# A block of ones for the key squares: one edit to the last layer and the mixers of a five-part network on one core

## The reference, cut to what matters

```python
# mixer: the differential heads' output is normalised per head (subln) before the output projection
o_d = _rmsnorm(o_d, subln) * (1.0 - lambda_init)
return jnp.concatenate([o_f, o_d], axis=-1) @ w_out

# last layer: 8 heads, q and k have 128 + 64 features; the 64 rotary ones of k are shared by all heads
u = rms_norm(x, norm_g) @ w_in
cq, ckv, kpe, z = jnp.split(u, ...)                     # 384, 256, 64, 1024
q = (rms_norm(cq, q_norm_g) @ w_uq).reshape(B, S, C_HEADS, QK_HEAD)
kv = (rms_norm(ckv, kv_norm_g) @ w_ukv)...              # k_nope, v
k = jnp.concatenate([k_nope, broadcast(kpe)], axis=-1)
q, k = rms_norm(q, qn_g), rms_norm(k, kn_g)             # over the 192 features of a head
# rotary turn of the last 64 features of q and k, then attention causal by chunks of 64
return x + (o * jax.nn.silu(z)) @ w_out
```

## Time and profile before

| | us |
|---|---|
| median of 3 runs (lowest, highest) | 2667.08 (2666.8, 2668.24) |
| the profiled execution | 2668.01 |
| its span, first to last instruction | 2666.2 |
| PE busy | 2648.1 |
| DVE busy | 1417.0 |
| ACT busy | 1015.8 |
| POOL busy | 187.7 |

### The profile page before, as it was taken

How to read it: one execution, slowest core, us unless ns; L and a number is a source line. 1 busy time by engine, 2 the same in 40 slices (tenths; PEclk the granted TensorE clock), 3 DMA queues, 4 the chain that set the end, 5 groups by cost and what they waited for, 6 DMA issues and landing times.

```text
span 2666.2 us, 33679 instructions
## 1 busy us (share of the span) xinstructions
PE 2648.1 (99%) x12646; PEld 2173.4 (82%) x12646; DVE 1417.0 (53%) x1946; ACT 1015.8 (38%) x1584; POOL 187.7 (7%) x140
## 2 busy tenths in 40 slices
PE   8999999999999999999999999999999999999999
PEld 7888887778888888888887878888887888888887
DVE  5444258785444235443268775444236657834443
ACT  4222135544222233232245643322135553324553
POOL 0000024101000010000043101000000000010000
PEclk9999999999999999999999999999999999999999
DMA  4322332113222222222232112222222222323111
GB/s 161 95 94 95 101 104 91 61 40 103 95 94 96 101 90 99 94 98 100 95 111 80 56 56 95 96 100 95 95 87 74 84 80 91 103 95 99 61 66 57
DMA packets 70326, 239.17 MB, mean 90 GB/s; under 512 B 8528, under 2 KB 10832, under 8 KB 70224
## 3 DMA queue, kind: packets, MB, share of 16 engines
q1 hardware_dynamic: 69792, 236.91, 26.7%
q10 hardware_dynamic: 432, 0.87, 0.1%
HBM read 230.15 MB, written 2.10 MB: 87 GB/s over the span
## 4 chain that ended last, share of the span: by engine, by line
PE 94%; DVE 4%; ACT 1%; issue 1%; DVEq 1%; DMA 0%; POOL 0%; ACTq 0%; SPq 0%
PE bank L400 21%; PE bank L402 21%; PE bank L401 21%; PE score L400 5%; PE score L401 5%; PE score L402 5%; PE flip_bank L400 2%; PE flip_bank L401 2%; PE flip_bank L402 2%; PE score L1146 1%; PE flip_bank L1169 1%; PE score L1857 1%; PE bank L2686 1%; PE score L2654 1%; DVE softstat L854 1%
## 5 line engine op out<-in xcount | busy, mean ns | idle before, releaser
L383 DVE TENSOR_TENSOR w_lo<-w_raw,w_hi 128x1024 fp32r<-128x1024 f32 x427 | 527.0, 1236 | 541.2 <-ACT w_hi L343 530.1
L400 PE MATMUL bank<-h_hi,w_hi 128*128 128x512 f32 x1856 | 742.7, 400 | 0.5 <-DVE w_lo L383 0.5
L402 PE MATMUL bank<-h_hi,w_lo 128*128 128x512 f32 x1856 | 724.0, 390 | 0.0
L401 PE MATMUL bank<-h_lo,w_hi 128*128 128x512 f32 x1856 | 723.2, 390 | 0.0
L343 ACT ACTIVATE w_hi<-w_raw 128x1024 fp32r<-128x1024 f32 x427 | 447.8, 1051 | 415.5 <-DMA w_raw<-stream 415.1
L400 PEld LDWEIGHTS bank<-h_hi,w_hi 128*128 128x128 f32 x1856 | 349.1, 188 | 73.7 <-issue 4.0
L402 PEld LDWEIGHTS bank<-h_hi,w_lo 128*128 128x128 f32 x1856 | 348.6, 188 | 74.0
L401 PEld LDWEIGHTS bank<-h_lo,w_hi 128*128 128x128 f32 x1856 | 349.3, 188 | 70.5 <-issue 2.4
L539 ACT ACTIVATE hid_hi<-tmp 128x512 f32 (+1 forms) x88 | 55.6, 632 | 408.6 <-DVE tmp L756 408.6
L750 DVE TENSOR_TENSOR tmp<-bank,rstd 128x512 f32<-128x512 f32 x132 | 91.1, 691 | 147.9 <-PE bank L402 147.6
L534 ACT ACTIVATE tmp<-tmp 128x512 f32<-128x512 f32 x88 | 55.6, 632 | 248.3 <-DVE tmp L750 248.3
(11 more groups left out here) (529 smaller groups left out, 3907.3 us busy)
## 6 DMA issues: line engine op xcount, KB each, us to landing
w_raw<-stream SPq DMA_DIRECT2D x427, 512.0 KB, 3.3
tmp<-tmp SPq DMA_DIRECT2D x64, 64.0 KB, 2.0
x_tok<-x SPq DMA_DIRECT2D x4, 512.0 KB, 6.6
wx_raw<-stream SPq DMA_DIRECT2D x4, 512.0 KB, 4.2
out<-out_tok SPq DMA_DIRECT2D x8, 256.0 KB, 2.0
tmp<-qr SPq DMA_DIRECT2D x16, 64.0 KB, 2.1
tab_in_f<-tables SPq DMA_DIRECT2D x1, 704.0 KB, 10.3
cos_sin<-rope ACTq DMA_DIRECT2D x1, 512.0 KB, 3.8
```

The source lines that it names most:

```text
L383: nc.vector.tensor_tensor(w_lo[:, s, :], w_raw[:, s, :], w_hi[:, s, :].bitcast(F32), ALU.subtract).then_inc(lo_ready, 1)
L400: nc.tensor.matmul(dst, whi, xhi, start=start, stop=False)
L401: nc.tensor.matmul(dst, whi, xlo, start=False, stop=False)
L402: return nc.tensor.matmul(dst, wlo, xhi, start=False, stop=stop)
```

## The change

In the last layer the sum of the key squares no longer goes by columns. POOL adds the shared part's squares to those of each head, cuts the result in a high and a low part, and PE multiplies both by the block of ones (`key_sums`), which leaves the sum on every partition and along the row. ACT takes the root of 128x512 (`key_roots`), DVE its reciprocal (`key_inverse`), and `keys` multiplies as before, with this tile in place of the spread one. The query columns stay; POOL adds the rotary squares before them, so `rope_sums` is gone, and they stand in one piece (`query_sums`), no longer beside the products of a unit. `z` 0 comes before `r` and `q` in `C_ORDER`. SP turns the second query tile of a pair of tiles two fetches later, and DVE rotates it later. ACT takes the roots ahead of the gates' function. The low halves of the output (`co_lo_pair`), `kpe_sq` and some small tiles lie elsewhere. In the mixers the roots of the first two differential heads are taken at step 16, that of the third there too; the reciprocals move from steps 21 to 28 to steps 18 to 25; the scan of the gates and its parts move from steps 7, 8, 11, 13 to 9, 11, 13, 14; and a part of the output projection is taken in another order.

The diff, cut to its core:

```diff
-        GATES_EXP, GATES_LOG, GATES_SUM, GATES_PARTS = 4, 5, 7, (8, 11, 13)
-        OUT_EARLY = [(m, kt) for m in range(3) for kt in (4, 5, 6, 0, 1, 7)] + [(m, 2) for m in range(3)]
+        GATES_EXP, GATES_LOG, GATES_SUM, GATES_PARTS = 4, 5, 9, (11, 13, 14)
+        OUT_EARLY = [(m, kt) for m in range(3) for kt in (4, 5, 6, 7, 0, 1)] + [(m, 2) for m in range(3)]
...
         def normed_at(k):
 
-            return {4 * 5 + 1: 0, 4 * 6: 1, 4 * 6 + 1: 2, 4 * 7: 3}.get(k)
-
-
-        INVERSE_AT = {21: (0, slice(0, S)), 22: (1, slice(0, P)), 23: (1, slice(P, 2 * P)), 24: (1, slice(2 * P, S)),
-                      25: (2, slice(0, S)), 26: (3, slice(0, P)), 27: (3, slice(P, 2 * P)), 28: (3, slice(2 * P, S))}
+            return {20: 0, 21: 1, 24: 2, 25: 3}.get(k)
+
+
+        INVERSE_AT = {18: (0, slice(0, P)), 19: (0, slice(P, 2 * P)), 20: (0, slice(2 * P, S)), 21: (1, slice(0, S)),
+                      22: (2, slice(0, P)), 23: (2, slice(P, 2 * P)), 24: (2, slice(2 * P, S)), 25: (3, slice(0, S))}
...
                         ins = nc.scalar.activation(d_var[:, g - 2, :], bank[7][:, :],
-                                                   ACT.Copy if g <= DIFF_HEADS else ACT.Sqrt,
-                                                   scale=1.0 / P, bias=0.0 if g <= DIFF_HEADS else small[:, 0:1])
+                                                   ACT.Copy if g < DIFF_HEADS else ACT.Sqrt,
+                                                   scale=1.0 / P, bias=0.0 if g < DIFF_HEADS else small[:, 0:1])
...
-                    if (g, b) == (DIFF_HEADS + 1, 0):
-                        nc.scalar.activation(d_var[:, 0:DIFF_HEADS - 1, :], d_var[:, 0:DIFF_HEADS - 1, :], ACT.Sqrt,
+                    if (g, b) == (DIFF_HEADS, 0):
+                        nc.scalar.activation(d_var[:, 0:2, :], d_var[:, 0:2, :], ACT.Sqrt,
                                              bias=small[:, 0:1]).then_inc(d_root, 1)
...
+                        if h == DIFF_HEADS - 1:
+                            dve.wait_ge(d_var_in, DIFF_HEADS * (layer + 1))
                         nc.vector.reciprocal(d_var[:, h, part], d_var[:, h, part])
...
-        C_ORDER = C_LATENT[QT:] + C_LATENT[:QT] + [("kv", 0), ("r", 0), ("q", 0), ("z", 0), ("z", 1)]
+        C_ORDER = C_LATENT[QT:] + C_LATENT[:QT] + [("kv", 0), ("z", 0), ("r", 0), ("q", 0), ("z", 1)]
...
+            def key_squares(u):
+                for j in range(2):
+                    pool.wait_ge(k_evac, 2 * u + j + 1)
+                    nc.gpsimd.tensor_tensor(k_sq[0:HEAD, j, :], k_sq[0:HEAD, j, :], kpe_sq[0:HEAD, :], ALU.add)
+                    pool.drain()
+                    nc.gpsimd.tensor_copy(k_sq_hi[k_at(u)][:, j, :], k_sq[:, j, :])
+                    pool.drain()
+                    nc.gpsimd.tensor_tensor(k_sq_lo[:, j, :], k_sq[:, j, :], k_sq_hi[k_at(u)][:, j, :].bitcast(F32),
+                                            ALU.subtract).then_inc(k_split, 1)
+
+            def query_squares(u):
+                if u % 2 == 0:
+                    pool.wait_ge(r_evac, u + 2)
+                for j in range(2):
+                    pool.wait_ge(q_evac, 2 * u + j + 1)
+                    rows = slice(HEAD * j, HEAD * j + HEAD)
+                    ins = nc.gpsimd.tensor_tensor(q_sq[rows, j, :], q_sq[rows, j, :], rope_sq[rows, u % 2, :], ALU.add)
+                ins.then_inc(q_added, 1)
+
+            key_squares(0)
+            query_squares(0)
+            for u in range(1, PAIRS):
+                query_squares(u)
+                key_squares(u)
...
+
+            def key_roots(u):
+                for j in range(2):
+                    act.wait_ge(k_summed, 2 * u + j + 1)
+                    nc.scalar.activation(k_root[k_at(u)][:, j, :], c_bank("ksum", 2 * u + j)[:, :], ACT.Sqrt,
+                                         scale=1.0 / QK_HEAD, bias=small[:, 1:2]).then_inc(k_rooted, 1)
...
                 if kind == "r":
+                    key_roots(0)
                     ropes(t)
...
                 if b == 2:
+                    if u < PAIRS - 1:
+                        roots(u + 1)
+                        key_roots(u + 1)
                     for t in (2 * u, 2 * u + 1):
                         act.wait_ge(z_evac, t + 1)
                         ins = nc.scalar.activation(zs[:, t, :], zs[:, t, :], ACT.Silu)
                     ins.then_inc(z_act, 1)
-                    if u < PAIRS - 1:
-                        roots(u + 1)
...
-                if i >= SLOTS and C_ORDER[i - SLOTS][0] == "r":
-                    for p in (2 * C_ORDER[i - SLOTS][1], 2 * C_ORDER[i - SLOTS][1] + 1):
+                for e in range(2):
+                    if i >= SLOTS + 2 * e and C_ORDER[i - SLOTS - 2 * e][0] == "r":
+                        p = 2 * C_ORDER[i - SLOTS - 2 * e][1] + e
                         sp.wait_ge(roped, p + 1)
                         sp.wait_ge(r_evac, p + 1)
                         turn(qr[:, p, :])
...
+            def query_sums(u):
+                dve.wait_ge(q_summed, u + 1)
...
+            def key_inverse(u, j):
+                dve.wait_ge(k_rooted, 2 * u + j + 1)
+                nc.vector.reciprocal(k_root[k_at(u)][:, j, :], k_root[k_at(u)][:, j, :])
+
             def keys(u):
+                dve.drain()
                 for j in range(2):
                     rows = slice(HEAD * j, HEAD * j + HEAD)
-                    dve.wait_ge(c_spread, 2 * u + j + 2)
-                    r = c_bank("spread", 2 * u + j)
+                    r = k_root[k_at(u)][:, j, :]
                     nc.vector.tensor_tensor(kr[rows, u % 2, :], kpe[rows, :], r[rows, :], ALU.mult)
-                    nc.vector.tensor_tensor(kn[:, u % 2, j, :], kn[:, u % 2, j, :], r[:, :], ALU.mult).then_inc(k_ready, 1)
+                    nc.vector.tensor_tensor(kn[:, u % 2, j, :], kn[:, u % 2, j, :], r, ALU.mult).then_inc(k_ready, 1)
...
+                if (kind, t) == ("z", 0):
+                    latent_means()
                 if kind == "r":
-                    latent_means()
+                    key_inverse(0, 0)
+                    key_inverse(0, 1)
                 if kind == "q":
-                    rope_sums(0)
+                    keys(0)
                     rope_query(0)
-                    rope_query(1)
                 if i == C_HEADS_AT - 1:
-                    key_query_sums(0)
+                    query_sums(0)
                     inverses(0)
-                    keys(0)
                 if kind == "z":
                     z_in(t)
             for k, (u, b) in enumerate(C_STEPS):
                 maxima(k)
                 if b == 3 and u < PAIRS - 1:
                     inverses(u + 1)
+                    keys(u + 1)
+                if b == 2 and u < PAIRS - 1:
+                    query_sums(u + 1)
                 for unit in C_UNITS_AT[k]:
                     dve_cut(C_START + c_unit(*unit) + 2)
                 tail = ((k - 4) // 4, (k - 4) // 2 % 2) if k >= 4 and k % 2 == 0 else None
                 if tail:
                     out_product(*tail)
-                if b == 3 and u < PAIRS - 1:
-                    keys(u + 1)
                 weigh(k)
+                if k == 0:
+                    rope_query(1)
+                if b == 2 and u < PAIRS - 1:
+                    key_inverse(u + 1, 0)
                 for kind, t in C_UNITS_AT[k]:
                     if kind == "z":
                         z_in(t)
                 if b == 2 and u < PAIRS - 1:
-                    key_query_sums(u + 1)
-                if k == TB + 1:
-                    rope_sums(1)
-                if k in (TB + 1, TB + 2):
-                    rope_query(k - TB + 1)
+                    key_inverse(u + 1, 1)
+                if k in (TB + 1, TB + 3):
+                    rope_query(2 if k == TB + 1 else 3)
                 if k == TB * 3:
                     dve_cut(C_OUT + 2)
...
+            def latent_sums():
+                dst = fresh("lat", 1)
+                pe.wait_ge(q_added, 1)
+                for b in range(TB):
+                    ins = column(dst, b, b, cq_sq[:, 0, :])
+                ins.then_inc(lat_summed, 1)
+
+            def query_sums(u):
+                dst = fresh("qsum", u)
+                pe.wait_ge(q_added, u + 2)
                 for j in range(2):
-                    spread(fresh("spread", 2 * u + j), k_inv(u, j)).then_inc(c_spread, 1)
+                    for b in range(TB):
+                        ins = column(dst, TB * j + b, b, q_sq[:, j, :])
+                ins.then_inc(q_summed, 1)
+
+            def key_sums(u):
+                for j in range(2):
+                    dst = fresh("ksum", 2 * u + j)
+                    pe.wait_ge(k_split, 2 * u + j + 1)
+                    nc.tensor.matmul(dst[:, :], ones_r[:, :], k_sq_hi[k_at(u)][:, j, :], start=True, stop=False)
+                    nc.tensor.matmul(dst[:, :], ones_r[:, :], k_sq_lo[:, j, :], start=False, stop=True).then_inc(k_summed, 1)
...
```

(71 more changed lines are left out.)

74 lines of the change are left out of this document (22 added, 52 removed).

## The result

The changed kernel takes 2653.26 us (median of five runs, 2650.89 to 2654.47) against 2666.89 us of the kernel before beside it (2666.72 to 2668.24). The ratio is 0.9947, with a 95% interval from 0.9936 to 0.9958: 13.6 us or 0.53% faster, where 20.8 us were forecast. 7.2 us are missing.

What follows compares the result with a forecast made beforehand. PE, busy 2648.1 of 2666.2 us, was taken as the bound. Last layer 16.6 plus mixers 4.5 less entry 0.3 gave 20.8 us: 2667.1 to 2646.3 us, low end 2643.4, high end 2652.8.

Steps and rivals of the forecast that it cites:

- the last layer with the entry: Last layer: 16.6 us saved by less PE work and a removed rotary-sum wait, less 0.3 us lost at the entry.
- the mixers: Mixers: earlier reciprocals remove PE's waits for key and transposed low halves, 4.5 us saved, bounds -1 and 5.7.
- PE's work in the last layer: Last layer: column sums and spreads removed, products through the ones added, net 16.1 us less on PE.
- Gathered in one piece: Last layer: 32 query columns, from 1.84 to 1.71 us a pair, with 4 latent columns 0.5 us less in all.
- my rivals: Five alternatives: mixers give nothing 0.15, DVE late at pair boundaries 0.12, POOL-DVE lock 0.08, slower 0.03, waits replace removed sums 0.02.
- Nothing gained, nothing lost: Last layer: turning the second query tile two fetches later and rotating it later costs nothing, bounds 1 us either way.
- I cost the boundary at nothing: Last layer's pair boundaries: DVE's added reciprocals delay PE by nothing, with 1.5 us to spare, 0.8 in two later pairs.
- Entry: Last layer's start: first query sums wait for POOL's addition, 0.3 us lost, bounds 0 and 1.
- The third rival: Last layer: POOL and DVE hold each other up, 6.8 us lost in four pairs, 2653.1 us; chance 0.08.
- for the scan of the gates: Mixers: 0.4 us of the 1.1 left in four small transpose waits saved, as the scan leaves a crowded step 7.

Runs made afterwards that it cites:

- e1: The changed kernel run once more, nothing edited: 2653.59 us, ratio 0.9951; no clock drop in its profiled execution.
- e7: Changed kernel with 64-column query sums, gates' scan back at step 7, and second-tile rotation, turn of x and DVE's query-sum wait moved later: 2647.5 us, ratio 0.9925.
- e12: Changed kernel with gates' scan back, rotation, turn of x and DVE's query-sum wait moved later, query sums still one column wide: 2648.13 us, ratio 0.993.
- e3: Changed kernel with 64 columns of ones instead of one through each block of query-square weights, still in one piece: 2651.81 us, ratio 0.9943.
- e8: Kernel before with only a pair's sixteen key and query columns gathered in one piece at the end of the z unit: 2675.73 us, single execution.
- e10: Changed kernel with the second query tile rotated on DVE after step 1's weighing instead of step 0's: 2655.42 us, single execution.
- e11: Changed kernel with the second turn of x moved behind the second z unit of its pair: 2651.41 us, single execution.
- e9: Changed kernel with the gates' scan and its parts back at steps 7, 8, 11, 13: 2652.16 us, single execution.
- e2: Changed kernel with the query columns back beside dense products, two behind each of four groups, instead of eight in a piece: 2656.49 us, ratio 0.9961.
- e5: Kernel before with only the mixers' part of the change (roots, reciprocals, gates' steps, early output order): 2665.98 us, ratio 0.9996.
- e4: Changed kernel with each of the eight query columns computed twice, a piece of sixteen: 2669.08 us, ratio 1.0007.
- e6: Kernel before with only the last layer's part of the change, mixers as before: 2655.34 us, ratio 0.9954.

## Where the prediction held, and where it missed

The direction was right, and the time came out 0.5 us above the top of the range. The 7.2 us missing come in three parts: 16.3 us forecast for the last layer with the entry, 261.87 - 248.15 = 13.7 had with the clock whole (2.6 missing); 4.5 forecast for the mixers, 2024.45 - 2022.93 = 1.5 had (3.0 missing); and what is left, 1.6 us, is what one drop of the clock costs; three of the changed kernel's five runs, the median one among them, have a mean clock of 0.999. The 2.6 us are made up, within the accuracy of the rows, of 0.6 for the gathered pieces, 0.8 for the rotation and 1.3 for the bank of z, as told below.

**PE's work in the last layer: right.** Forecast 16.1 us, 15.8 had (PE's busy time of before less that of e1). The products through the ones follow each other at the forecast distance, as PE's timeline of the changed kernel shows:

```profile
2526.84 0.39 PE L2656 MATMUL bank<-k_sq_hi,ones_r 128*128 128x512 f32 x1
...
2527.06 0.39 PE L2657 MATMUL bank<-tmp_r,ones_r 128*128 128x512 f32 x1
```

**"Gathered in one piece", 0.5 us less: the term that was mis-sized.** The piece takes 1.78 us to the next product, 0.22 a column and not the 0.20 of the earlier trace rows, and the product behind is longer by the 0.09 us: 1.87 us a pair where I forecast 1.71, four times 0.16 more, and the spread columns took 1.84. So even at the full clock gathering gained nothing. The larger error is that I took PE's price for granted at the full clock. A drop costs 1.5 to 1.6 us (e1 against the first execution; e7 against e12, 4.8 us for three), and one execution has none to three of them: up to 5 us more, where I had put 0.5 less. None of my rivals had the clock in it. All rows I read were of stretches at 1.00, and none of them had such a piece of eight: the four columns of the earlier trace rows are half as many, and the eight-product spread of the earlier trace rows, as long as the piece, passes 128 columns a product. The rows show PE busy in the whole piece before the clock falls; e3, e8 and e12 tie the fall to the piece and to its narrowness. The Trainium skill (TensorE: Matmul & The Clock Gate, What's actually happening) says that the gate sets the clock by how busy PE has been recently, and lowers it when PE is idle. The rows here have it fall behind a piece in which PE is recorded as busy without a gap, so by the measurement recorded busy time is no proof against it.

**"Nothing gained, nothing lost", transfers: 0.8 lost,** inside the bounds of 1 us. ACT, DVE and POOL on the changed kernel's timeline, at the rotation of the second tile:

```profile
2468.22 0.69 DVE L2360 TENSOR_TENSOR qr<-qr,rot 128x512 f32<-128x512 f32 x1 [0.62 <-DMA tmp<-qr]
2468.60 1.43 POOL L2152 TENSOR_TENSOR q_sq<-q_sq,rope_sq 64x512 f32<-64x512 f32 x1 [11.07 <-ACT qn L2185]
2468.83 1.76 DVE L2361 TENSOR_TENSOR tmp<-tmp,rot 128x512 f32<-128x512 f32 x1
...
2470.59 1.28 POOL L2152 TENSOR_TENSOR q_sq<-q_sq,rope_sq 64x512 f32<-64x512 f32 x1 [0.55 <-ACT qn L2185]
2470.66 1.76 DVE L2363 TENSOR_TENSOR qr<-qr,tmp 128x512 f32<-128x512 f32 x1
2472.34 0.68 DVE L2426 TENSOR_REDUCE softstat<-score 128x2 f32<-128x512 f32 x1
2473.30 0.57 ACT L2238 ACTIVATE c_probs<-score,softstat,m_cols 128x256 f32<-128x256 f32 x1 [1.84 <-DVE softstat L2429]
...
2474.88 0.69 ACT L2208 ACTIVATE kn<-bank,cols 128x512 f32<-128x512 f32 x1
```

The rotation waits 0.62 us for its transfer; then two products of 0.69 us take 1.76 us each, beside POOL's additions. The maxima of step 1 are behind them on DVE, ACT's exponentials wait for these (1.84 us), the key is evacuated behind the exponentials, and its bank is the next that PE wants. With the rotation a step later (e10) the 0.8 us come back. I had named the queue ("with the maxima of step 1 queued behind it") and not followed it to PE.

**"I cost the boundary at nothing": right for what it says, and one consumer missed.** PE's list of waits has none of the scores for the keys. In the pair of the earlier trace rows DVE ends its last key product at 2497.1 and PE begins the scores at 2498.9, 1.8 us to spare where I had 1.5. But the reciprocals also stand ahead of `z_in`, which frees the bank of z. DVE and PE of the changed kernel at step 10:

```profile
2568.74 3.35 DVE L2409 RECIPROCAL k_root<-k_root 128x512 f32<-128x512 f32 x1 [2.59 <-ACT k_root L2228]
...
2572.01 0.63 DVE L2421 TENSOR_TENSOR zs<-bank,rstd 128x512 f32<-128x512 f32 x1
...
2572.69 0.66 PE L2730 MATMUL bank<-tab,x 128*128 128x128 f32 x4 [1.10 <-DVE zs L2421]
```

The last pair is the only one with a turn of x behind it, and the turn takes that bank. With e11's order 1.3 us come back. I followed the first pair's boundary only.

**Entry: 0.3 us forecast, 0.26 lost, but at another place, so by luck.** The wait that I forecast, of the first query sums for POOL's addition, did not come: on the changed kernel's timelines the addition ends at 2457.53 and the sums start at 2457.68. What PE lost it lost before that, at the first pair's key sums:

```profile
2445.97 0.47 PE L2656 MATMUL bank<-k_sq_hi,ones_r 128*128 128x512 f32 x1 [0.26 <-POOL tmp_r L2143]
...
2456.16 1.37 POOL L2152 TENSOR_TENSOR q_sq<-q_sq,rope_sq 64x512 f32<-64x512 f32 x1 [0.34 <-ACT qn L2185]
```

**The third rival is there, mostly at other places.** POOL and DVE do stretch each other, as the rows of the rotation show, and the first pair's chain on POOL took longer than in the earlier trace rows (2.09 and 2.26 us against 1.29). That gave the 0.26 us, the only listed wait of a sum through the ones for POOL; in the other pairs the cover held.

**The mixers: the named waits went, and the 0.4 us "for the scan of the gates" were a loss.** With the scan back the forecast of 4.5 us is nearly met: 2024.45 - 2020.41 = 4.0. Moving it and its parts from step 7 to step 9 and later costs 2.5 us of that. DVE and POOL of the changed kernel at step 9:

```profile
460.51 1.56 POOL L487 TENSOR_TENSOR tmp<-tmp,cos_sin 128x512 f32<-128x512 f32 x1 [0.89 <-DMA tmp<-tmp]
460.99 2.16 DVE L818 TENSOR_TENSOR_SCAN negcum<-gate_rows 8x512 f32<-8x512 f32 x1
462.04 5.04 POOL L488 TENSOR_TENSOR tmp<-tmp,cos_sin 128x512 f32<-128x512 f32 x1
```
and the same two operations with the scan at step 7 (e9):
```profile
451.84 1.21 DVE L818 TENSOR_TENSOR_SCAN negcum<-gate_rows 8x512 f32<-8x512 f32 x1
...
464.92 2.27 POOL L488 TENSOR_TENSOR tmp<-tmp,cos_sin 128x512 f32<-128x512 f32 x1
```

At step 9 the scan meets POOL's rotation of the next key: 2.16 instead of 1.21 us for the scan, and 5.04 instead of 2.27 for the key's second product. On DVE the maxima of the next scores stand behind the scan, and PE waits 0.51 us for the probabilities made from them and later for their low halves. No wait of PE in this stretch is put down to POOL. I had weighed the lock for the last layer and not for the mixers, where the change moves a DVE operation as well.

Not settled: why a given execution has none or three drops with the same instructions, and how narrow or long a piece must be. Only 1 and 64 columns, and pieces of eight and sixteen, were run, and 64 columns also write more results, which no run separates. The mean clock is a rough sign, too: it was 0.999 in two of e2's runs and one of e5's, which were not profiled and have no piece. In profiled executions it also falls in the last microseconds, as PE's work ends (0.96 from 2655 us to the end in before).

## What to carry to other kernels

Price a moved operation by everything queued behind it on its engine, down to the bank that each frees, and at every repetition of the pattern: the last is often the one with another consumer. When DVE work with two inputs in SBUF is moved, look what POOL does at the new place. And when small products are gathered in one piece, look at the granted clock behind it in several executions before counting the gain; more columns through the same weights cost here next to nothing.

## What the runs showed of the hardware

- Eight (or, in e4 and e8, sixteen) FP32 products of one column in a piece, with PE recorded as busy, were followed in some executions by a stretch at 1.2 GHz, which cost 1.5 to 1.6 us behind a piece of eight. Of the nine profiled executions with a narrow piece (the changed kernel, e1, e4, e6, e8 to e12) seven show such a stretch, each time behind a piece; of the five without one (before, e2, e3, e5, e7) none does. Of the 23 runs with the narrow piece of eight fourteen had a mean clock under 1.00, of the ten with 64 columns through the same weights (e3, e7) none, at 1.97 against 1.92 us a piece.
- A POOL product took 5.04 us beside a row of DVE operations and 2.27 us at the same place in e9; a like one at 431.18 us took 1.28. What the prediction cites from the Trainium skill (SBUF - State Buffer, Who interferes with whom), that the second waits until the first ends, gives a wait of one operation. That POOL lost to several in a row is how I read these rows; no experiment separated it from other causes.
